# The chunk loop of an RWKV-7 mixer: block-diagonal operands against 64x64 tiles

## What is computed

```python
def step(state, inp):
    r_t, w_t, k_t, v_t, kk_t, a_t = inp
    sa = jnp.einsum('bhvk,bhk->bhv', state, -kk_t)
    state = (state * w_t[:, :, None, :]
             + sa[..., None] * (kk_t * a_t)[:, :, None, :]
             + v_t[..., None] * k_t[:, :, None, :])
    return state, jnp.einsum('bhvk,bhk->bhv', state, r_t)
```

## Time and profile before

| what | value |
|---|---|
| time, median of 3 runs | 2004.44 us (2001.65 to 2006.21) |
| profiled execution, its time | 2007.96 us |
| profiled execution, its span | 2006.2 us |
| instructions | 25559 |
| PE busy | 1958.1 us (98%) |
| DVE, ACT, POOL busy | 1013.0, 766.2, 216.0 us |
| mean granted clock of TensorE | 0.991 |

### The profile page before, as it was taken

The page is one execution under the profiler, slowest core; times in us unless marked ns, Lnnn a source line. Parts: engine busy times, 40 slices in busy tenths (PEclk is TensorE's granted clock), DMA queues, the critical chain, the costliest instruction groups (busy, mean ns, idle before and its releaser), DMA issues.

```text
span 2006.2 us, 25559 instructions
## 1 busy us (share of the span) xinstructions
PE 1958.1 (98%) x10043; PEld 1603.6 (80%) x10043; DVE 1013.0 (50%) x1359; ACT 766.2 (38%) x1156; POOL 216.0 (11%) x262
## 2 busy tenths in 40 slices
PE   8999999999999999999999999999989999999998
PEld 6876788888888777888888888777889777888887
DVE  6445544333426756444433425759553456666533
ACT  3226542222224465542222323454544444333423
POOL 3000010000002302010000001203652000000001
PEclk9999899999999999999999999999999999999999
DMA  5310023323222201023223232320110223232231
GB/s 172 112 52 1 27 84 105 105 84 105 91 98 76 68 22 64 22 87 105 93 95 104 85 105 84 103 91 29 22 43 19 88 74 105 84 105 91 98 105 63
DMA packets 137773, 158.64 MB, mean 79 GB/s; under 512 B 15960, under 2 KB 125536, under 8 KB 137696
## 3 DMA queue, kind: packets, MB, share of 16 engines
q1 hardware_dynamic: 136256, 155.01, 24.2%
q0 software_dynamic: 1440, 2.58, 0.5%
HBM read 153.89 MB, written 3.68 MB: 79 GB/s over the span
## 4 chain that ended last, share of the span: by engine, by line
PE 86%; DVE 8%; ACT 3%; issue 2%; DMA 0%; POOL 0%; SPq 0%; DVEq 0%; ACTq 0%; POOLq 0%
PE bank L2761 33%; PE bank L2794 16%; PE bank L2378 13%; PE bank L2403 3%; PE bank L2453 3%; PE bank L2483 3%; PE bank L2812 2%; PE bank L2469 1%; DVE XL L1564 1%; DVE w_lo L1557 1%; PE bank L2707 1%; PE bank L2740 1%; PE bank L2431 1%; PE bank L2561 1%; PE bank L3025 1%
## 5 line engine op out<-in xcount | busy, mean ns | idle before, releaser
L2761 PE MATMUL bank<-XH,w_hi 128*128 128x512 f32 x992 | 387.7, 391 | 2.6 <-DVE w_lo L1850 1.9
L2761 PE MATMUL bank<-XL,w_hi 128*128 128x512 f32 x992 | 386.6, 390 | 0.0
L2761 PE MATMUL bank<-XH,w_lo 128*128 128x512 f32 x992 | 386.4, 390 | 0.0
L2761 PEld LDWEIGHTS bank<-XH,w_hi 128*128 128x128 f32 x992 | 186.6, 188 | 42.0 <-DVE w_lo L1850 2.4
L2761 PEld LDWEIGHTS bank<-XL,w_hi 128*128 128x128 f32 x992 | 186.7, 188 | 39.3 <-issue 0.5
L2761 PEld LDWEIGHTS bank<-XH,w_lo 128*128 128x128 f32 x992 | 186.7, 188 | 39.0
L2378 PE MATMUL bank<-XH,w_hi 128*128 128x512 f32 x504 | 200.1, 397 | 4.8 <-DVE w_lo L1557 2.5
L2378 PE MATMUL bank<-XH,w_lo 128*128 128x512 f32 x504 | 196.4, 390 | 0.0
L2378 PE MATMUL bank<-XL,w_hi 128*128 128x512 f32 x504 | 196.2, 389 | 0.0
L1557 DVE TENSOR_TENSOR w_lo<-w_raw,w_hi 128x2048 fp32r<-128x2048 f32 (+4 forms) x65 | 118.1, 1834 | 93.3 <-ACT w_hi L1026 92.9
L1026 ACT ACTIVATE w_hi<-w_raw 128x2048 fp32r<-128x2048 f32 (+5 forms) x66 | 98.3, 1510 | 120.3 <-PE bank L2378 50.0
(11 more groups left out here) (430 smaller groups left out, 3505.7 us busy)
## 6 DMA issues: line engine op xcount, KB each, us to landing
w_raw<-in_ffn_w_gate SPq DMA_DIRECT2D x22, 1024.0 KB, 5.3
w_raw<-in_ffn_w_up SPq DMA_DIRECT2D x22, 1024.0 KB, 5.3
w_raw<-in_ffn_w_down SPq DMA_DIRECT2D x22, 1024.0 KB, 4.9
w_raw<-in_w_up SPq DMA_DIRECT2D x22, 1024.0 KB, 5.1
w_raw<-in_w_in SPq DMA_DIRECT2D x13, 1024.0 KB, 5.2
w_raw<-in_w_down SPq DMA_DIRECT2D x11, 1024.0 KB, 4.9
w_raw<-in_even_w_in SPq DMA_DIRECT2D x9, 1024.0 KB, 5.3
w_raw<-in_even_w_out SPq DMA_DIRECT2D x4, 1024.0 KB, 5.3
```

Source lines behind the costliest of these rows:

```text
L2761: m = pe.matmul(bank[b][:, :], w[:, k, P * c:P * (c + 1)], x[:, k, :], start=(k == 0 and j == 0), stop=(k == KT - 1 and j == 2))
```

## The change

Nothing is block-diagonal in the loop any more, apart from `XTbd`. P, U, the state and the turned operands are kept as 4 pairs of 64 rows by 64 columns, one head on each half of the partitions, and every product on them is two matmuls on 64x64 tiles, one per head. The turns are products with the unit matrix: data as the stationary operand, `ident` as the moving one; V and A go into one bank and are copied out in one operation, KK into another, with a second buffer. The two products of the inverse are matmuls of 32 rows by 32 columns. The block copies on ACT (`blocks`) and POOL (`key_rows`) and the memsets that cleared them are gone; `inner_rows` copies the off-diagonal blocks of all chunks at the start, chunk 0 and chunks 1 to 7. On PE the U products of the state and of y go behind the parts that do not need U, and the wait for U's copy goes with them. The indentation of the lines is shortened here.

```diff
--- before.py
+++ after.py
@@ -492,26 +490,20 @@
 outer = NS.rearrange("p a b -> p (a b)")

 taken[0] = base2
-KVbd_flat = region(1024)
-KKRbd_flat = region(1024)
-KVbd, KKRbd = (x.rearrange("p (a b c) -> p a b c", a=2, c=P) for x in (KVbd_flat, KKRbd_flat))
-region(512)
-region(4 * NCH * BL)
-region(512)
+KV = region(512, 2, 4, CH)
+KKtok = region(512, 2, 4, CH)
+Vc = region(4 * CH, 4, CH)
+Toff = region(4 * BL, 4, BL)
+taken[0] = base2 + 4096
 late_xt = region(2048)
 AR = region(1024, 2, 2, 4 * CH)
-Sbd = region(1024, 2, 4, P)
-pair_tiles = under_split[:, 0:2048]
-AAbd, KKbd, Vbd, Toff = (pair_tiles[:, 512 * i:512 * (i + 1)].rearrange("p (a b) -> p a b", b=P) for i in range(4))
+S = region(512, 2, 4, CH)
 XTbd = [x.rearrange("p (a b) -> p a b", b=P) for x in (under_split[:, 4096:6144], late_xt)]
-AAtok = rstd.rearrange("p (a b) -> p a b", b=P)
-Pn = NS[:, 0, :].rearrange("p (a b) -> p a b", b=P)
-Ubd = NS[:, 1, :].rearrange("p (a b) -> p a b", b=P)
+Pn, U = (NS[:, i, 0:4 * CH].rearrange("p (a b) -> p a b", b=CH) for i in range(2))
 taken[0] = base0
-Aoff = region(512, 4, P)
-bonus_in = region(512)[:, 0:4 * CH].rearrange("p (a b) -> p a b", b=CH)
-Vtok = region(1024, 2, 4, P)
-KKtok = region(512, 4, P)
+Aq = region(NCH * 4 * BL, NCH * 4, BL)
+bonus_in = region(4 * CH, 4, CH)
+VAtok = region(1024, 2, 2, 4, CH)
 taken[0] = base0
...
@@ -822,7 +817,7 @@
     else:
         if u == first["mix_out"]:
             inverse_blocks()
-            sp.wait_ge(rw_al, NCH)
+            sp.wait_ge(rw_al, 2)
...
@@ -951,18 +945,10 @@
         pool.wait_ge(inv_solved, 2)
         g0 = ATT["diff"]["g0"]
         pool.wait_ge(at_s, g0 + 15)
-        link(pool.memset(KKRbd_flat, 0.0))
...
         pool.wait_ge(rw_vc, 4)
-
-        def key_rows(c):
-            if c >= 2:
-                pool.wait_ge(rw_p, c - 1)
-            link(pool.tensor_copy(KKRbd[side(0), c % 2, :, side(0)], KRk[side(0), :, chunk(c)]))
-            pool.tensor_copy(KKRbd[side(1), c % 2, :, side(1)], KRk[side(1), :, chunk(c)]).then_inc(rw_kbd, 1)
-            pool.wait_ge(rw_kbd, c + 1)

         def bonus(c):
             if c >= 1:
...
             if c >= 1:
-                pool.wait_ge(rw_turn, 3 * c - 2)
-            link(pool.tensor_copy(Vbd[side(0), :, side(0)], vv[side(0), :, chunk(c)]))
-            pool.tensor_copy(Vbd[side(1), :, side(1)], vv[side(1), :, chunk(c)]).then_inc(rw_vbd, 1)
+                pool.wait_ge(rw_turn, 2 * c - 1)
+            pool.tensor_copy(Vc, vv[:, :, chunk(c)]).then_inc(rw_vbd, 1)
             pool.wait_ge(rw_vbd, c + 1)

-        def inner_rows(c):
-            if c == 0:
-                pool.wait_ge(rw_ak, 4)
-            else:
-                pool.wait_ge(rw_t, c)
-            link(pool.tensor_copy(Aoff[quarter(0), :, quarter(1)], Ak[quarter(0), 4 * c:4 * c + 4, quarter(1)]))
-            pool.tensor_copy(Aoff[quarter(2), :, quarter(3)], Ak[quarter(2), 4 * c:4 * c + 4, quarter(1)])\
-                .then_inc(rw_al, 1)
-            pool.wait_ge(rw_al, c + 1)
+        def inner_rows(first, last):
+            for h in range(2):
+                m = pool.tensor_copy(Aq[quarter(2 * h), 4 * first:4 * last, :],
+                                     Ak[quarter(2 * h), 4 * first:4 * last, quarter(1)])
+                if h == 0:
+                    link(m)
+            m.then_inc(rw_al, 1)

         value_rows(0)
         pool.wait_ge(at_t, g0 + 24)
         bonus(0)
-        link(pool.memset(Aoff, 0.0))
-        inner_rows(0)
-        key_rows(0)
+        inner_rows(0, 1)
+        pool.wait_ge(rw_al, 1)
+        inner_rows(1, NCH)
+        pool.wait_ge(rw_al, 2)
...
-    def blocks(c):
-        if c >= 1:
-            act.wait_ge(rw_turn, 3 * c)
-        for h in range(2):
-            act.activation(AAbd[side(h), :, side(h)], aa[side(h), :, chunk(c)], ACT.Copy)
-            m = act.activation(KKbd[side(h), :, side(h)], kk[side(h), :, chunk(c)], ACT.Copy)
-        m.then_inc(rw_bd, 1)
...
-            m = act.activation(Toff[quarter(2 * h + 1), :, quarter(2 * h)],
-                               pairs(bank[7][quarter(2 * h + 1), 0:P]), ACT.Copy, scale=-1.0)
+            r = quarter(2 * h + 1)
+            m = act.activation(Toff[r, :, :], pairs(bank[7][r, 0:4 * BL]), ACT.Copy, scale=-1.0)
         m.then_inc(rw_tl, 1)
...
     def token_major(c):
-        for i, to in enumerate((Vtok[:, c % 2, :, :], AAtok, KKtok)):
-            act.wait_ge(rw_turn, 3 * c + i + 1)
-            if c >= 1:
-                if i == 0 and c >= 2:
-                    act.wait_ge(rw_y, c - 1)
-                if i == 1:
-                    act.wait_ge(rw_s, c)
-            act.activation(to, pairs(bank[(6, 4, 5)[i]][:, :]), ACT.Copy).then_inc(rw_tok, 1)
+        act.wait_ge(rw_turn, 2 * c + 1)
+        if c >= 2:
+            act.wait_ge(rw_y, c - 1)
+        act.activation(VAtok[:, c % 2, :, :, :].rearrange("p a t d -> p (a t d)"), bank[6][:, :],
+                       ACT.Copy).then_inc(rw_tok, 1)
+        act.wait_ge(rw_turn, 2 * c + 2)
+        act.activation(KKtok[:, c % 2, :, :], compact(5), ACT.Copy).then_inc(rw_tok, 1)
...
-        act.activation(Pn, pairs(bank[0][:, :]), ACT.Copy, scale=-1.0).then_inc(rw_pc, 1)
+        act.activation(Pn, compact(0), ACT.Copy, scale=-1.0).then_inc(rw_pc, 1)
...
-        act.activation(Ubd, pairs(bank[1][:, :]), ACT.Copy).then_inc(rw_uc, 1)
+        act.activation(U, compact(1), ACT.Copy).then_inc(rw_uc, 1)
...
-        if c + 2 < NCH:
-            blocks(c + 2)
...
@@ -2260,22 +2224,20 @@
         dve.wait_ge(rw_a2, c + 1)
         if c >= 2:
             dve.wait_ge(rw_y, c - 1)
-        incl = C("incl").unsqueeze(1).broadcast_to([P, 4, CH])
+        incl, strict = (C(n).unsqueeze(1).broadcast_to([P, 4, CH]) for n in ("incl", "strict"))
         by_key = pairs(bank[5][:, :])
-        for h in range(2):
-            dve.tensor_tensor(KVbd[side(h), c % 2, :, side(h)], by_key[side(h), :, CH:2 * CH],
-                              C("strict")[side(h), :].unsqueeze(1).broadcast_to([CH, 4, CH]), ALU.mult)
-        dve.tensor_tensor(pairs(AR[:, c % 2, 0, :]), pairs(bank[4][:, 0:4 * CH]), incl, ALU.mult)
+        dve.tensor_tensor(KV[:, c % 2, :, :], by_key[:, :, CH:2 * CH], strict, ALU.mult)
+        dve.tensor_tensor(pairs(AR[:, c % 2, 0, :]), compact(4), incl, ALU.mult)
         dve.tensor_tensor(pairs(AR[:, c % 2, 1, :]), by_key[:, :, 0:CH], incl, ALU.mult)
         y = vv[:, :, chunk(c)]
         dve.wait_ge(rw_vbd, c + 1)
-        dve.tensor_tensor(y, y, pairs(bank[4][:, 4 * CH:8 * CH]), ALU.mult).then_inc(rw_am, 1)
+        dve.tensor_tensor(y, y, compact(4, 4 * CH), ALU.mult).then_inc(rw_am, 1)

...
-            new = Sbd[:, (c + 1) % 2, :, :]
-            rate = fac[:, :, c:c + 1].broadcast_to([P, 4, P])
+            new = S[:, (c + 1) % 2, :, :]
+            rate = fac[:, :, c:c + 1].broadcast_to([P, 4, CH])
             dve.wait_ge(rw_s, c + 1)
             if c == 0:
-                dve.tensor_tensor(new, pairs(bank[2][:, :]), rate, ALU.mult).then_inc(rw_st, 1)
+                dve.tensor_tensor(new, compact(2), rate, ALU.mult).then_inc(rw_st, 1)
             else:
-                link(dve.tensor_tensor(new, Sbd[:, c % 2, :, :], pairs(bank[2][:, :]), ALU.add))
+                link(dve.tensor_tensor(new, S[:, c % 2, :, :], compact(2), ALU.add))
                 dve.tensor_tensor(new, new, rate, ALU.mult).then_inc(rw_st, 1)
         if c == NCH - 1:
...
@@ -3000,14 +2962,18 @@
     def part(t, n=CH):
         return slice(n * t, n * (t + 1))

+    sides = [side(0), side(1)]
+
     def keys(c):
-        pe.wait_ge(rw_bd, c + 1)
-        if c >= 1:
-            pe.wait_ge(rw_tok, 3 * c)
+        if c == 0:
+            pe.wait_ge(rw_rk, 4)
+            pe.wait_ge(rw_keys, 4)
+        else:
+            pe.wait_ge(rw_tok, 2 * c)
         for t in range(4):
-            for r in (side(0), side(1)):
+            for r in sides:
                 pe.matmul(bank[4][r, part(t)], aa[r, t, chunk(c)], KRr[r, t, chunk(c)], start=True, stop=True)
-            for r in (side(0), side(1)):
+            for r in sides:
                 pe.matmul(bank[5][r, part(t, P)].rearrange("p (a b) -> p a b", a=2), kk[r, t, chunk(c)],
                           KRrk[r, :, t, chunk(c)], start=True, stop=True)
         pe.wait_ge(rw_bq, c + 1)
@@ -3017,22 +2983,30 @@
         pe.wait_ge(rw_vbd, c + 1)
         if c == 0:
             pe.wait_ge(at_on, ATT["diff"]["h0"] + 8)
+        else:
+            pe.wait_ge(rw_tok, 2 * c - 1)
+        for t in range(4):
+            for r in sides:
+                pe.matmul(bank[6][r, part(t)], Vc[r, t, :], ident[r, r], start=True, stop=True)
+            for r in sides:
+                m = pe.matmul(bank[6][r, part(4 + t)], aa[r, t, chunk(c)], ident[r, r], start=True, stop=True)
+        m.then_inc(rw_turn, 1)
         pe.wait_ge(rw_am, c + 1)
-        for i, src in enumerate((Vbd, AAbd, KKbd)):
-            if i == 0 and c >= 1:
-                pe.wait_ge(rw_tok, 3 * c - 2)
```

(66 more changed lines are left out.)

19 lines of the change are left out of this document (5 added, 14 removed).

## The result

The changed kernel takes **1979.17 us** (median of 4 runs, 1977.33 to 1980.99) against 2004.68 (4 runs, 2001.65 to 2006.21): a ratio of 0.988, 95% interval 0.9866 to 0.9895. It is 25.5 us faster; 21.7 had been forecast, and 1982.7 us. The profiled execution took 1980.99 us, its span 1979.0 (before 2006.2).

A forecast was written before the change was run, and what follows sets the result against it. TensorE's own queue was taken as the bound. Six loop periods (16.4 us), the beginning (3.6) and the end (1.7) sum to 21.7 us off, giving 1982.7 us against the median 2004.44; range 1976 to 1996.

The forecast's parts named there:

- Prices: Assumed TensorE costs in the chunk loop: 0.115 us per 64x64 or 32x32 pair, 0.15 us per change of tile size.
- 32x32 pair: Off-diagonal and inverse products: taken at 0.115 us a pair, between bounds of 0.06 and 0.40; no row showed one.
- Does anything else become the bound?: Check of each wait in the new loop order against the work covering it; copies of 256 columns on ACT about 0.38 us.
- thinnest cover: P's wait for the V and A copy, 0.85 us after their turns, under KK turn and inverse, 1.07 us.
- Beginning: Start of the chunk loop: P(0) about 1.0 us sooner, U(0) 2.1 sooner, U(0) to turn(1) 5.0 us; gain 3.6 us.
- End: After turn(7): shorter turns, inverse and P (4.13 to 3.06 us) and shorter copies before ACT's split; gain 1.7 us.
- Sum: Whole kernel: 16.4 us from six loop periods, 3.6 at the beginning, 1.7 at the end, 21.7 us in all.
- (a): Rival: small tiles or size changes in the loop are dearer, chunk 10.1 us, 1993 us, at the far end some 2003; 17%.
- (b): Rival: small pieces cost 0.06 a pair, no cost around them, clock kept at the start; period about 8.1, 1976 us; 6%.
- (c): Rival: TensorE is granted half clock through the loop of half-used array, 16.5 us a chunk at worst, 2040 us; 7%.
- (d): Rival: the 40 new pairs a chunk don't overlap in one bank, 4.2 us more a chunk, 2014 us; 3%.
- (e): Rival: a wait called covered opens (V and A copy, POOL's bonus), 0.5 us a chunk, 1987 us; within the forecast's 66%.

The follow-up runs named there:

- the experiment with the heads apart: Changed kernel with 64x64 products outside keys issued for all even heads, then all odd, instead of head beside head: 2002.61 us, ratio 0.9997 to the kernel before.
- the two with the stand: Changed kernel with mix_out's split by the fourth chunk, 1980.09 us; the same plus late inner_rows copy, bonus on 64x64 tiles and filler products, 1974.33 us.

## Why the prediction was right

Direction, mechanism and size held; each term, by its name there:

- **Prices.** 64x64 pairs at 0.115: right in P, U, state, turns and y, seven pieces within 0.02. The change of size at 0.15: right where P follows the inverse (0.26 instead of 0.12) and in U. **The 32x32 pair was the mis-sized term**: 0.115 taken, 0.062 measured, next to the lower bound 0.06. The step that failed was "off-diagonal's passes with 32 moving columns (0.10) are hardly cheaper than passes with 128": those rows were passes on the whole array, and I carried them over to another tile size. With the same 32 moving columns a pass took 0.10 us there and 0.031 on a 32x32 tile (0.062 for the two passes of each of two tiles), so what had held those passes up was not the number of moving columns but something that shrinks with the tile; the weights, 128 columns there and 32 here, are the obvious suspect, and no run separates them from the rest. The Trainium skill (TensorEngine Tiling, Instruction Overhead) says that a small moving operand costs as much as one of about 60 columns; read in columns this trace disagrees, since 32 moving columns on 32x32 tiles cost 0.062 where 64 on 64x64 tiles cost 0.115. The Trainium skill gives the overhead in the same section as about 60 cycles too, which at 2.4 GHz is 25 ns (an estimate from that figure). That is less than the 31 ns of a pass here, so read in cycles nothing here contradicts it. The two pieces make 0.48 us a chunk, which is all that the period is below 8.70 (0.42; four other pieces came out 0.01 to 0.02 longer each), and 2.5 us in six periods: 18.9 instead of 16.4.
- **Does anything else become the bound?** No. The thinnest cover held by little: in one steady chunk ACT's copy of V and A ended 0.12 us before P began. The 256-column copies took 0.38 on ACT and 0.42 on DVE, as estimated.
- **Beginning.** 3.6 forecast, 2.8 measured. "P(0) comes about 1.0 us sooner" was wrong: it didn't move. The inner_rows copies on POOL were costed only as work with a cover and for what queues behind them on POOL. They cost through the engine beside them, which had to wait for them: 0.74 and 0.32 us on two DVE operations on the path, 1.06 in all, just the gain that had been forecast. Moving the long copy gave 1.39 us back at P(0). U(0) came 1.1 sooner, not 2.1, and at 1482.3 only because the whole run lay 1.5 us earlier.
- **End.** 1.7 forecast, 2.3 measured. The split set the end as said (ACT 1541.17, DVE 1543.11, gate product 1545.91). Of the 0.6 more, 0.2 are the cheaper inverse, and 0.4 lie between P's end and the split, 1.47 us where 1.85 had been estimated.
- **Sum.** 21.7 forecast. The stretch gave 24.0: 2.5 more from the steady chunks, 0.8 less at the beginning, 0.6 more at the end. The medians differ by 25.5.
- **Rivals.** (a), dearer small tiles: measured the other way. (b), cheaper small pieces: its price came true, its free changes and its kept clock did not, so the period was 8.28 and not 8.1 (and its two figures don't belong together: by the prediction's own terms a period of 8.1 gives 1977.6 us, and 1976 needs 7.8). (c), the clock gate: the steady windows are at 1.00; half clock stood only behind stands of PE, as in the kernel before. (d), no overlap in one bank: the Trainium skill (TensorEngine Tiling, Gotcha 1: PSUM Pressure) says that different row tiles cannot access the same bank at the same time. The pair rows of 0.12 and the experiment with the heads apart, where a lone product costs as much as a pair, show the opposite. (e), a covered wait opens: not in the loop, but at the beginning, by the slower DVE.

**Open**: why TensorE stood in the last y piece. That it goes when the second load is held back is shown in two kernels, and that a packet of the instruction queue came late in the two with the stand; that TensorE waited for this packet is inferred. That DVE and POOL wait for each other is read from starts and ends; through what they get in each other's way no run shows.
